# Block products of a hybrid decoder step: operand rows moved to multiples of 128 bytes

## The reference

```python
xn = rmsnorm(x)
u, v, q, k, va, ga, gb = split(xn @ w_in)               # gelu on u and v
a = u * (tril(W_s) @ rmsnorm(v) + b)                    # chunks of 128 tokens
b = sliding-window attention with sinks and ALiBi       # 16 heads, 4 kv heads, window 128
h = sigmoid(ga) * (a @ w_oa) + sigmoid(gb) * (b @ w_ob)
x = x + h @ w_out
y = rmsnorm(x + relu(rmsnorm(x) @ w_up)**2 @ w_down)    # w_up 1024x4096, w_down 4096x1024
```

## Time and profile before

| | |
|---|---|
| median of three runs | 1535.7 us |
| the profiled execution, its span | 1535.4 us |
| TensorE matmul busy | 1519.2 us, 99% |
| weight loads busy | 1491.0 us, 97% |
| VectorE busy | 1074.5 us, 70% |
| ScalarE busy | 764.5 us, 50% |
| GpSimd (POOL) busy | 192.5 us, 13% |
| mean granted TensorE clock | 0.998 |

### The profile page before, as it was taken

How to read it: one execution, slowest core, us unless ns; L and a number is a source line. 1 busy time by engine, 2 the same in 40 slices (tenths; PEclk the granted TensorE clock), 3 DMA queues, 4 the chain that set the end, 5 groups by cost and what they waited for, 6 DMA issues and landing times.

```text
span 1535.4 us, 28799 instructions
## 1 busy us (share of the span) xinstructions
PE 1519.2 (99%) x12186; PEld 1491.0 (97%) x12186; DVE 1074.5 (70%) x1445; ACT 764.5 (50%) x1153; POOL 192.5 (13%) x195
## 2 busy tenths in 40 slices
PE   8999999999999999999999999999999999999998
PEld 7988989999999999999999999999999999999997
DVE  7676565315686786857688777867697669776975
ACT  6565555425536645565434745335543454335533
POOL 7132232100000410000010300000000000000001
PEclk9999999999999999999999999999999999999999
DMA  9611011317695344545697376454544545454512
GB/s 252 204 58 30 29 31 30 97 42 199 196 302 153 100 111 111 148 121 145 152 234 200 103 149 168 111 155 95 163 111 143 133 138 138 131 135 115 157 28 111
DMA packets 109495, 200.65 MB, mean 131 GB/s; under 512 B 19696, under 2 KB 47344, under 8 KB 102040
## 3 DMA queue, kind: packets, MB, share of 16 engines
q1 hardware_dynamic: 92008, 128.74, 25.4%
q0 software_dynamic: 9840, 62.94, 21.3%
q10 hardware_dynamic: 7520, 7.14, 1.5%
HBM read 121.81 MB, written 19.30 MB: 92 GB/s over the span
## 4 chain that ended last, share of the span: by engine, by line
PE 96%; DVE 2%; issue 0%; DMA 0%; ACT 0%; POOL 0%; SPq 0%; DVEq 0%
PE ps L1788 73%; PE ps L1532 14%; PE ps L1520 3%; PE ps L1618 2%; PE ps L1600 2%; PE ps L1558 1%; PE ps L1766 1%; DVE y_t L1509 1%; DMA x_stage<-in_x_prompt 0%; DVE k_lo L1132 0%; POOL prob L630 0%; PE ps L1684 0%; PE ps L1706 0%; PE ps L1540 0%; DVE prob L1156 0%
## 5 line engine op out<-in xcount | busy, mean ns | idle before, releaser
L1788 PE MATMUL ps<-xp_lo,wp_hi 128*128 128x258 f32 x3136 | 888.9, 283 | 0.0
L1788 PE MATMUL ps<-xp_hi,wp_hi 128*128 128x258 f32 x3136 | 886.1, 283 | 0.8 <-ACT gate_b L771 0.5
L1788 PE MATMUL ps<-xp_hi,wp_lo 128*128 128x258 f32 x3136 | 882.8, 282 | 0.0
L1788 PEld LDWEIGHTS ps<-xp_hi,wp_hi 128*128 128x128 f32 x3136 | 593.9, 189 | 1.5 <-ACT gate_b L771 0.8
L1788 PEld LDWEIGHTS ps<-xp_hi,wp_lo 128*128 128x128 f32 x3136 | 593.6, 189 | 0.0
L1788 PEld LDWEIGHTS ps<-xp_lo,wp_hi 128*128 128x128 f32 x3136 | 591.7, 189 | 0.0
L771 ACT ACTIVATE wp_hi<-wbuf 128x1024 fp32r<-128x1024 f32 x196 | 208.0, 1061 | 530.1 <-PE ps L1788 529.9
L1272 DVE TENSOR_TENSOR wp_lo<-wbuf,wp_hi 128x1024 fp32r<-128x1024 f32 x196 | 244.3, 1246 | 155.0 <-ACT wp_hi L771 155.0
L1532 PE MATMUL ps<-xn_hi,w_hi 128*128 128x344 f32 x456 | 150.7, 331 | 0.0
L1532 PE MATMUL ps<-xn_hi,w_lo 128*128 128x344 f32 x456 | 145.6, 319 | 0.0
L1532 PE MATMUL ps<-xn_lo,w_hi 128*128 128x344 f32 x456 | 145.6, 319 | 0.0
(11 more groups left out here) (208 smaller groups left out, 1579.5 us busy)
## 6 DMA issues: line engine op xcount, KB each, us to landing
wbuf<-wbuf POOLq DMA_DIRECT2D x57, 1024.0 KB, 7.5
wbuf<-in_w_up SPq DMA_DIRECT2D x24, 1024.0 KB, 5.2
wbuf<-in_w_down SPq DMA_DIRECT2D x24, 1024.0 KB, 5.1
wbuf<-in_w_in SPq DMA_DIRECT2D x18, 1024.0 KB, 5.5
raw<-in_w_in SPq DMA_DIRECT2D x38, 256.0 KB, 3.3
wbuf<-in_w_ob SPq DMA_DIRECT2D x6, 1024.0 KB, 7.9
wbuf<-in_w_oa SPq DMA_DIRECT2D x6, 1024.0 KB, 4.9
wbuf<-in_w_out SPq DMA_DIRECT2D x6, 1024.0 KB, 6.9
```

The lines of the kernel that those rows point to most:

```text
L1788: last = mm(ps[:, 2 * p + b, 0:HN], w[:, (2 * n + p // 2) % 2, k, p % 2 * P:(p % 2 + 1) * P], x[n % 2][:, k, b * HN:(b + 1) * HN], start=( ...
```

## The change

The tiles `xp_hi` and `xp_lo` get a padded form: each row of 516 floats becomes two halves of 288 floats, 1152 bytes or nine times 128, of which 258 are used. The tiles and several other regions are placed at multiples of 128 bytes, so that each of the 258-column rows starts at one. The writes by ScalarE and VectorE and the reads by TensorE follow the new shape; the numbers computed, their order, the counts of instructions and all waits are as before. The tiles are larger (9216 bytes in place of 8256), and to make room the reserve in SBUF for the descriptors of POOL's DMAs is set to 8192 bytes per partition, half of what it was.

```diff
+        def aligned(offset):
+            return (offset + 127) // 128 * 128
-        def region(nbytes):
-            start = at[0]
+        def region(nbytes, whole=False):
+            start = aligned(at[0]) if whole else at[0]
...
+        XB = aligned(4 * HN) // 4
+        XPB = 4 * MH * 2 * XB
-        r_0, r_0b, r_1, r_2, r_3 = (region(ACTB) for _ in range(5))
+        r_0, r_0b, r_1, r_2 = (region(ACTB, whole=True) for _ in range(4))
+        r_3 = region(2 * XPB + 8 * MH * MW + 4 * NB * HPG, whole=True)
...
-            (r_3 + 8 * MH * HT + 4 * MH * MW + 4 * NB * HPG, r_3 + 8 * MH * HT, r_0b, r_0b + 4 * MH * MW, r_raw))]
+            (r_3 + 2 * XPB + 4 * MH * MW + 4 * NB * HPG, r_3 + 2 * XPB, r_0b, r_0b + 4 * MH * MW, r_raw))]
...
-        r_s = region(4 * T + 8 * MH * HT)
+        r_s = region(aligned(4 * T) + 2 * XPB, whole=True)
...
-        xp_hi = [place(f"xp_hi{n}", [P, MH, HT], F32R, at_) for n, at_ in enumerate((r_3, r_s + 4 * T))]
-        xp_lo = [place(f"xp_lo{n}", [P, MH, HT], F32R, at_ + 4 * MH * HT) for n, at_ in enumerate((r_3, r_s + 4 * T))]
+        xp_hi = [place(f"xp_hi{n}", [P, MH, 2, XB], F32R, at_) for n, at_ in enumerate((r_3, r_s + aligned(4 * T)))]
+        xp_lo = [place(f"xp_lo{n}", [P, MH, 2, XB], F32R, at_ + XPB) for n, at_ in enumerate((r_3, r_s + aligned(4 * T)))]
+        def xp_half(x, half):
+            return x[:, 2 * half:2 * half + 2, :, 0:HN]
+        def by_bank(x):
+            return x.rearrange("p k (b t) -> p k b t", b=2)
...
-                copy(xp_hi[n % 2][:, 2 * half:2 * half + 2, :], x_source(g, i, half)).then_inc(xp_hi_ready, 1)
+                copy(xp_half(xp_hi[n % 2], half), by_bank(x_source(g, i, half))).then_inc(xp_hi_ready, 1)
...
-                tt(xp_lo[n % 2][:, two, :], x_source(n // 7, n % 7, half), xp_hi[n % 2][:, two, :].bitcast(F32),
+                tt(xp_half(xp_lo[n % 2], half), by_bank(x_source(n // 7, n % 7, half)), xp_half(xp_hi[n % 2], half).bitcast(F32),
...
-                                      x[n % 2][:, k, b * HN:(b + 1) * HN], start=(first and k == 0 and m == 0),
+                                      x[n % 2][:, k, b, 0:HN], start=(first and k == 0 and m == 0),
...
-    nc = bacc.Bacc("TRN2", target_bir_lowering=False, num_devices=1)
+    nc = bacc.Bacc("TRN2", target_bir_lowering=False, num_devices=1, dynamic_dma_scratch_size=8192)
```

More of the change, by code:

```diff
@@ L96, in build_trunk @@
         at = [(nc.sbuf_base + 31) // 32 * 32]
-        def region(nbytes):
-            start = at[0]
-            at[0] += (nbytes + 31) // 32 * 32
+        def aligned(offset):
+            return (offset + 127) // 128 * 128
+        def region(nbytes, whole=False):
+            start = aligned(at[0]) if whole else at[0]
+            at[0] = start + (nbytes + 31) // 32 * 32
             assert at[0] <= nc.sbuf_usable_end, at[0]
@@ L113, in build_trunk @@
         ACTB = KT * T * 4
-        r_0, r_0b, r_1, r_2, r_3 = (region(ACTB) for _ in range(5))
+        HT = T // 2
+        HN = HT // 2
+        MH = KT // 2
+        MW = MH * P
+        XB = aligned(4 * HN) // 4
+        XPB = 4 * MH * 2 * XB
+        r_0, r_0b, r_1, r_2 = (region(ACTB, whole=True) for _ in range(4))
+        r_3 = region(2 * XPB + 8 * MH * MW + 4 * NB * HPG, whole=True)
         xn_hi = place("xn_hi", [P, KT, T], F32R, r_0)
@@ L162, in build_trunk @@
         assert o + 4160 <= r_3 + 8 * KT // 2 * T // 2 + 4 * (KT // 2 * P) * 4 + 4 * P
-        r_raw, r_whi, r_wlo = (region(2 * KT * P * 4) for _ in range(3))
+        r_raw, r_whi, r_wlo = (region(2 * KT * P * 4, whole=True) for _ in range(3))
         raw = place("raw", [P, 2, KT, P], F32, r_raw)
@@ L1274, in x_low @@
             def x_low(n, half):
-                two = slice(2 * half, 2 * half + 2)
                 dve.wait_ge(xp_hi_ready, 2 * n + half + 1)
-                tt(xp_lo[n % 2][:, two, :], x_source(n // 7, n % 7, half), xp_hi[n % 2][:, two, :].bitcast(F32),
+                tt(xp_half(xp_lo[n % 2], half), by_bank(x_source(n // 7, n % 7, half)), xp_half(xp_hi[n % 2], half).bitcast(F32),
                    ALU.subtract).then_inc(xp_split, 1)
```

## The result

The kernel after takes 1545.65 us (median of four runs, 1545.31 to 1546.82), the kernel before 1535.81 in the same runs. The ratio is 1.0062, with a 95% interval of 1.005 to 1.0074: slower, and outside of what the measurement leaves open. The profiled execution has a span of 1543.9 us, 8.5 more than before.

The account below looks back on a forecast made before the run. TensorE's 9408 block-product matmuls at 119.8 ns were taken as the bound. Only the moving rows counted: 1535.4 - 5.6 = 1529.8 us of span, with the median 0.3 above, so 1530 us; range 1518 to 1547.

Parts of the forecast that it names:

- What bounds the kernel: TensorE busy 99% of the span; block products take 9408 matmuls times 119.8 ns, 1127 us, and only that distance matters.
- the excess of 12.3 ns: Block-product step of 119.8 ns over the array's 107.5; 116 us over 9408 matmuls, all that operand addresses can reach.
- The writes of x: ScalarE and VectorE write four pieces instead of one; nothing taken, at most 27 us without the cover of their waits.
- the DMA reserve: Halved reserve for POOL's accumulating DMAs; nothing taken, at most 7.5 us delay per matrix product, covered by POOL's waits.
- Rival D: Late writes of x or POOL DMAs make TensorE wait; no chance of its own beyond a part of the slower 0.27.
- The moving rows: TensorE's reads of x in the block products: 0.6 ns a step gained, 5.6 us; bounds 17 us gained, 11 us lost.
- The first comparison: Halves of an even block product's column block, even against odd multiples of 8 bytes: both 1.44 us, so misalignment to 16 costs nothing.
- the scores: Attention matmuls with half their rows aligned: 118.3 ns a step, excess 11.7 in place of 12.3, so 0.6 ns less.
- Rival B: Moving row and weight load start in step at multiples of 128 bytes, excess up to 13.5 ns: 1547 us; chance 0.27, shared.
- Rival A: Excess paid by the piece or fixed per weight change, so the mean step stays: 1535.7 us, give or take 3; chance 0.29.
- Rival C: Whole excess comes from rows straddling multiples of 128: step to some 110 ns, gain 92 us, 1443 us; chance 0.04.

Follow-up runs that it names:

- reserve_only: Kernel before with only the reserve for POOL's DMA descriptors halved to 8192 bytes: 1536.37 us, ratio 1.0002.
- m5_bases: Block product's matmuls alone, without the layer: eight row layouts, each at twelve pairs of starts of x tiles and weights; steps from 117.5 to 122 ns.
- m1_addresses: Matmuls alone, without the layer, in stretches of 64 with equal addresses, over a table of x row and weight starts: 116.6 to 122.2 ns at 258 columns.
- shift_8: Kernel after with the 258 columns 8 bytes further on in each padded row: 1526.47 us, ratio 0.9938.
- halves_1040: Kernel after with each row starting 104 bytes in and the two halves 1040 bytes apart, not 1152: 1527.08 us, ratio 0.9943.

## Why the prediction was wrong

*What bounds the kernel* held: only the distance of starts moved, and it explains the difference to a fraction of a microsecond. That the excess of 12.3 ns is all that addresses can reach held as well; the layouts tried moved it between 10 and 14.5 ns.

*The writes of x* and *the DMA reserve* were put at nothing and are nothing: the low x takes 1234 ns (before 1232), ScalarE's cover is 538.7 us (before 529.9), `reserve_only` has the time of before. Rival D did not happen. In the sum, the 0.3 us from span to median hide two terms that nearly cancel: a time lies 1.7 us above its span (1545.59 and 1543.9 for the kernel after), and the profiled execution of before was 1.5 us long by its stretch at half the clock.

*The moving rows* is the step that failed. I took a gain of 0.6 ns; it was a loss of 1.04 ns, which the bounds (1.8 gained to 1.2 lost) held and the chosen value had with the wrong sign. The failure is in how the rows were read. The first comparison took the equal halves of 1.44 us for a sign that being off a multiple of 16 bytes costs nothing. But 0.01 us of a timeline is 0.8 ns a step over twelve steps, more than the whole term; to the nanosecond the two halves take 1.434 and 1.446 us, 1.0 ns a step apart, in the kernel before and in m5_bases alike. From the scores, with every other row at a multiple of 128, I inferred that aligned rows are cheap; from the odd block products' 2.86 us that a uniform layout would end at the better phase. But the step does not belong to a row. It belongs to the repeating sequence: row starts, distance to the weights, what came before. The scores have other columns, weights and order, and the stream alone gives 116.6 to 122.2 for one row read again and again. Neither row could give a sign, and the forecast should have stayed at the mean with both sides open.

*Rival B* had the direction and nearly the size (1547 against 1545.65), its reason only in part. The size is luck: it was taken from the 344-column matmuls of the first part, and m1_addresses has those at 156.0 to 160.0 ns, an excess of 12.7 to 16.6, by the address of x alone. Nor did the two operands ever start in step, as B had it: half of the rows of the kernel after are 128 bytes off in the 256. The distance of x and weights does matter, and it is the distance: moving x by 128 bytes or the weights by 128 gives the same step in m5_bases. So the two reads do meet somewhere. But equal starts are not the worst case, and an excess of 10.4 or 18.5 ns with a quarter of the weight load says that it is not simply the weight load in the way.

*Rival A* was right in one thing: the count of pieces does not change, and the mean over many layouts, 119.8 ns, is the step of before. A given layout lies above or below it, and no rule found here tells beforehand which: after is at +1.0, shift_8 at -0.9. *Rival C* did not come near: the lowest step of 244 layouts is 117.5, not 110.

By the Trainium skill, "SBUF — State Buffer", section "Door 1: The DMA port swizzle", the count of 16-byte lines would leave the time unchanged; measured is 1545.65 against 1535.81, and 42 us between layouts with the same count of 65. The runs decide against it as the whole account. The equal halves that were said to agree with it are not equal. What stays open is the mechanism: no run here tells which part of TensorE's reads takes the 10 to 14 ns, why 256 bytes is the period of the distance, or why a stretch can have two rhythms.

## What to carry to other kernels

Where a kernel is bound by back-to-back matmuls, the addresses of the moving rows and of the weights can be worth about 2% of the matmuls' step either way (117.5 to 121.9 ns around 119.8), here 1.5% of the kernel's time less or 1.3% more, and alignment is not the rule: measure the repeating sequence alone, with the kernel's own distances modulo 256 bytes, over a hundred layouts in one run, and take the best. A forecast for such an edit from single neighbouring rows has no sign. And a stream that leaves out everything but the matmuls is only a stand-in if it keeps every address that counts: here the base of the tiles was the one left out. A comparison of two stretches says something only where the effect is larger than the digits of the view: over twelve steps a hundredth of a microsecond is 0.8 ns a step.

## What the runs showed of the hardware

- The step of a stream of 258-column matmuls, each with a weight load, is the same to 0.1 ns in a bare stream and in the full kernel with DMAs, VectorE and ScalarE at work (120.83 and 120.84, 118.90 and 118.90, 121.9 and 121.9); the largest difference at the kernel's own distances is 0.15 (119.0 and 118.9, halves_1040).
- The excess over the array's time shrinks little or not at all with the weight load: from 128 to 32 weight columns it goes from 12.5 to 10.2 ns at 258 moving columns (9.2 to 8.5 with x 16 bytes on), and from 13.3 to 18.4 at 512 (18.3 to 18.7), by the trace's start times. It is gone at half the clock.
- From 128 to 240 columns the stream with x and weights at 0 stays at 111.7 to 112.0 ns a step (with x 8 bytes on, 240 columns take 116.6); from 256 to 264 it is at 118.7 to 120.8, and from 272 on it follows the columns with 12 to 16 ns on top.
- In five of eight layouts the step depends on the distance of x and weights modulo 256 bytes, by up to 2.9 ns. In the other three, whose halves lie 1152 bytes apart, the same move exchanges the fast and the slow half and leaves the mean (1.441 and 1.461 us for twelve matmuls, then 1.461 and 1.446).
- The same sequence of addresses can run in two rhythms: 120.0 and 120.8 ns for one pair of addresses in m1_addresses, 119.2 and 121.9 for the 1040 layout in m5_bases.
